# Two transformer blocks on one core: the raw residual stream is transposed, the norms' factors move to the weights and to the copies

## The reference

```
rms_norm(x, g) = x * rsqrt(mean(x * x) + 1e-6) * g
first block:  h = rms_norm(x, g_pre_mix);   proj = h @ w_in      (1024 x 3072)
              mix = [causal attention | gated retention] @ w_out
              x = x + rms_norm(mix, g_post_mix)
              c = cross_attention(rms_norm(x, g_pre_cross), rms_norm(mem, g_mem))
              x = x + rms_norm(c, g_post_cross)
              h = rms_norm(x, g_pre_ffn); gu = h @ w_gate_up; f = (silu(gate) * up) @ w_down  (2816 wide)
              x = x + rms_norm(f, g_post_ffn)
second block, layer 0: mix = [top-64 sparse attention chosen by an index | short convolution] @ w_out
              layer 1: mix = latent attention: q and kv pass through ranks 384 and 256 with norms of their own
              both:    x = x + rms_norm(mix, post);  x = x + rms_norm(relu(rms_norm(x, pre) @ w1)^2 @ w2, post)   (4096 wide)
```

## Time and profile before

| what | value |
|---|---|
| timed runs | 1163.12, 1163.36 and 1167.18 us, median 1163.36 |
| span of the profiled execution, first to last instruction | 1162.1 us |
| PE busy with products | 1066.5 us, 92% of the span |
| DVE, ACT, POOL busy | 638.6 (55%), 509.1 (44%), 99.7 us (9%) |
| mean granted clock of TensorE | 0.967 of full speed |
| PE on the chain that ended last | 73% |
| read from memory | 179.28 MB, 155 GB/s over the span |

### The profile page before, as it was taken

How to read it: one execution, slowest core, us unless ns; L and a number is a source line. 1 busy time by engine, 2 the same in 40 slices (tenths; PEclk the granted TensorE clock), 3 DMA queues, 4 the chain that set the end, 5 groups by cost and what they waited for, 6 DMA issues and landing times.

```text
span 1162.1 us, 13304 instructions
## 1 busy us (share of the span) xinstructions
PE 1066.5 (92%) x5072; PEld 886.6 (76%) x5072; DVE 638.6 (55%) x783; ACT 509.1 (44%) x637; POOL 99.7 (9%) x128
## 2 busy tenths in 40 slices
PE   5998899988999997899978799999878897999997
PEld 4887688776888886778867688888777776888886
DVE  4577663465554454457685655455545856454552
ACT  4556443344444444244444444444434644444441
POOL 1010110000000001102740000000140000000000
PEclk9999999998999999699989899999989998999999
DMA  8642274124545545434323545554154225455520
GB/s 340 249 182 91 74 263 170 73 91 163 201 162 191 205 158 179 144 147 144 145 72 109 197 166 183 197 192 150 52 175 150 74 86 188 179 180 183 188 100 36
DMA packets 29418, 180.92 MB, mean 156 GB/s; under 512 B 3520, under 2 KB 3904, under 8 KB 10816
## 3 DMA queue, kind: packets, MB, share of 16 engines
q1 hardware_dynamic: 26064, 170.08, 40.2%
q0 software_dynamic: 2592, 9.96, 2.5%
q10 hardware_dynamic: 720, 0.30, 0.1%
HBM read 179.28 MB, written 1.05 MB: 155 GB/s over the span
## 4 chain that ended last, share of the span: by engine, by line
PE 73%; DVE 12%; ACT 6%; POOL 5%; issue 3%; DMA 1%; POOLq 0%; DVEq 0%; ACTq 0%
PE PS L1257 63%; PE PS L1301 3%; DVE w_lo L827 3%; DVE h L905 3%; ACT w_hi L515 2%; PE PS L1346 2%; ACT work L576 2%; PE PS L1419 2%; PE PS L1329 2%; POOL h L431 1%; DVE x L920 1%; POOL rstd L408 1%; POOL msq L407 1%; DMA gain<-in_gains 1%; POOL arena L424 1%
## 5 line engine op out<-in xcount | busy, mean ns | idle before, releaser
L827 DVE TENSOR_TENSOR w_lo<-w_raw,w_hi 128x2048 fp32r<-128x2048 f32 (+3 forms) x177 | 369.1, 2096 | 317.3 <-ACT w_hi L515 316.9
L515 ACT ACTIVATE w_hi<-w_raw 128x2048 fp32r<-128x2048 f32 (+3 forms) x177 | 309.0, 1750 | 255.0 <-PE PS L1257 252.1
L1257 PE MATMUL PS<-w_hi,hT_hi 128*128 128x512 f32 (+3 forms) x904 | 323.1, 398 | 27.0 <-DVE hT_lo L843 17.7
L1257 PE MATMUL PS<-w_lo,hT_hi 128*128 128x512 f32 (+3 forms) x904 | 316.1, 391 | 0.0
L1257 PE MATMUL PS<-w_hi,hT_lo 128*128 128x512 f32 (+3 forms) x904 | 315.5, 390 | 0.0
L1257 PEld LDWEIGHTS PS<-w_hi,hT_hi 128*128 128x128 f32 x904 | 171.6, 194 | 64.3 <-issue 13.6
L1257 PEld LDWEIGHTS PS<-w_hi,hT_lo 128*128 128x128 f32 x904 | 173.6, 193 | 34.2
L1257 PEld LDWEIGHTS PS<-w_lo,hT_hi 128*128 128x128 f32 x904 | 174.1, 194 | 32.9
L1257 PE MATMUL PS<-w_hi,gT_hi 128*128 128x512 f32 x408 | 126.2, 391 | 0.6 <-DVE w_lo L827 0.6
L1257 PE MATMUL PS<-w_hi,gT_lo 128*128 128x512 f32 x408 | 125.7, 389 | 0.0
L1257 PE MATMUL PS<-w_lo,gT_hi 128*128 128x512 f32 x408 | 125.7, 389 | 0.0
(11 more groups left out here) (134 smaller groups left out, 739.4 us busy)
## 6 DMA issues: line engine op xcount, KB each, us to landing
w_raw<-in_w SPq DMA_DIRECT2D x64, 1024.0 KB, 4.8
w_raw<-in_w_gu SPq DMA_DIRECT2D x22, 1024.0 KB, 4.8
w_raw<-in_w_in SPq DMA_DIRECT2D x12, 1024.0 KB, 6.3
w_raw<-in_w_dn SPq DMA_DIRECT2D x22, 512.0 KB, 4.7
gain<-in_gains POOLq DMA_DIRECT2D x16, 512.0 KB, 4.8
w_raw<-in_w_out SPq DMA_DIRECT2D x4, 1024.0 KB, 4.8
w_raw<-in_w_mem_k SPq DMA_DIRECT2D x4, 1024.0 KB, 4.8
w_raw<-in_w_mem_v SPq DMA_DIRECT2D x4, 1024.0 KB, 4.8
```

Source lines behind the costliest of these rows:

```text
L515: act.activation(w_hi[:, u % RING, 0:size], w_raw[:, u % RAW, 0:size], ACT.Copy).then_inc(w_high, 1)
L827: dve.tensor_tensor(w_lo[:, u % RING, 0:size], w_raw[:, u % RAW, 0:size], w_hi[:, u % RING, 0:size].bitcast(F32), ALU.subtract).then_inc(w ...
L1257: mm = pe.matmul(bank(t, j)[:, 0:width], rows[:, kc0 + k, tok], w[:, s, at:at + width], start=begin and i == 0, stop=end and i == 2)
```

## The change

- The raw rows of `x` are transposed, 512 columns as soon as they are added up (`turn_stream`), not normed rows `h`. `normed` is gone, for `mem` too.
- A norm's gain is a factor of a row of the weights. The split multiplies by it: ACT's copy has it as a scale for each partition, DVE's subtraction becomes `(raw * gain) - hi`. Each block of 128 rows has its own column of gains in `gcol`, so a unit is split in `kcs` instructions: two of 1024 columns in most projections, four of 512 in the `up` units. Units without a norm before them (`w_out`, `w_co`, `w_dn` and their like) stay as they were.
- The 16 gains are loaded as 16 rows of one tile; PE transposes them at the start and ACT copies nine of them to `gcol`. The other seven, the gains behind a block, are still spread by POOL's queue.
- The reciprocal root is a factor of a token. It goes into the copies of the accumulators, into SiLU and ReLU as scale, and into the product of gate and up. These copies wait for `rstd_ready`.
- `add_to_stream` works in halves of 512 columns. In a boundary `high_rows` now comes before `stream_square`, and splits have other places between the steps.
- The start: SP loads x tile 0, half of the first unit, x tile 1, the other half; the first group has five units (1, 1, 2, 2, 2 blocks) and goes unit by unit over both tiles (`first_project`). The squares of x stand behind the first two splits.
- Behind a hidden layer the transposes of tile 0 stand ahead of the last part of its products; the transposes of tile 1 ahead of the fourth unit of the next projection, not behind it. The index queries now come before the index projection. The first `turn_hidden` of a layer stands between the second chunk's two units.
- The output is stored in four halves, not two tiles. `mem` is loaded ahead of `decay`.

```diff
-            def split(u, size, it=None):
+            def split(u, it=None):
...
-                act.activation(w_hi[:, u % RING, 0:size], w_raw[:, u % RAW, 0:size], ACT.Copy).then_inc(w_high, 1)
+                size, kcs, col = UNITS[u]
+                w = size // kcs
+                for k in range(kcs):
+                    ins = act.activation(w_hi[:, u % RING, k * w:(k + 1) * w], w_raw[:, u % RAW, k * w:(k + 1) * w], ACT.Copy,
+                                         scale=1.0 if col is None else gcol[:, col + TURNED * k:col + TURNED * k + 1])
+                ins.then_inc(w_high, 1)
...
+                    if col is None:
+                        ins = dve.tensor_tensor(lo, raw, hi, ALU.subtract)
+                    else:
+                        ins = dve.scalar_tensor_tensor(out=lo, in0=raw, scalar=gcol[:, col + TURNED * k:col + TURNED * k + 1], in1=hi,
+                                                       op0=ALU.mult, op1=ALU.subtract)
...
+            def add_to_stream(b, t):
...
+                dve.wait_ge(rstd_ready, stat + 1)
+                for i in range(2):
+                    cols = slice(512 * i, 512 * i + 512)
+                    steps.link(dve.scalar_tensor_tensor(out=h[:, t, cols], in0=PS[:, 2 * t + i, :], scalar=rstd[:, stat:stat + 1],
+                                                        in1=gain[:, g, cols], op0=ALU.mult, op1=ALU.mult))
+                    dve.tensor_tensor(x[:, t, cols], x[:, t, cols], h[:, t, cols], ALU.add).then_inc(x_ready, 1)
...
             def boundary_after(m):      # ACT
...
                 split_to(e + 1)
+                high_rows(hT_hi, 0)
                 stream_square(0)
-                high_rows(hT_hi, 0)
+                split_to(e + 2)
                 wait_acc(1)
                 square(acc(1))
-                split_to(e + 2)
-                stream_square(1)
                 split_to(e + 3)
                 high_rows(hT_hi, 1)
+                stream_square(1)
...
-            project(1, 8, [80], copies=2, rows=rows, hooks={(1, 0): tile1})
-            project(4, 2, wide, copies=2)
+            project(4, 2, wide, copies=2, rows=rows, hooks={(0, 3): tile1})
+            project(1, 8, [80], copies=2)
...
+            def turn_stream(t):
+
+                for half in range(2):
+                    n["x"] += 1
+                    pe.wait_ge(x_ready, n["x"])
+                    turn([x[:, t, P * (4 * half + b):P * (4 * half + b + 1)] for b in range(4)])
```

More of the change, by code:

```diff
@@ L49, with gained, plain_units, hidden_units @@
-SIZES, FIRST = [], {}
+GAINS = 16
+PRE_ROWS = [slice(0, 2), slice(3, 12, 2), slice(12, 15, 2)]
+PRE = {name: g for g, name in enumerate(["pre_mix", "mem", "pre_cross", "pre_ffn", "mix_pre0", "ffn_pre0", "mix_pre1", "ranks", "ffn_pre1"])}
+TURNED = len(PRE)
+def gained(gain, count, kcs, size):
+    return [(size, kcs, PRE[gain] + TURNED * j * kcs) for j in range(count)]
+def plain_units(count, size=2048):
+    return [(size, 1, None)] * count
+def hidden_units(gain, chunks, down):
+    up, down = gained(gain, 2, 4, 2048), plain_units(2, down)
+    return up + (up + down) * (chunks - 1) + down
@@ L50, with added @@
+UNITS, FIRST = [], {}
 for _name, _units in SCHEDULE:
[L51 to L56, removed]
+    FIRST[_name] = len(UNITS)
+    UNITS += _units
+COUNT = len(UNITS)
+POST = [2, 4, 6, 8, 10, 13, 15]
 GAIN_SLOTS = 2
+LATENTS = 4 + 4 * 5
+RETENTION = 34
+def added(b, t):
+    if b == 6:
+        return LATENTS + 8 + t
+    return 4 + 4 * b + 2 * t + (4 if b == 5 else 0)
@@ L343, in plain, with first_rows @@
                     for j in range(groups.shape[1]):
+                        if g == 0 and j < skip:
+                            continue
                         load(u, groups[g, j])
                         u += 1
+            def first_rows():
+                for t in range(TT):
+                    sp.dma_start(x[:, t, :], A["x"][:, t, :]).then_inc(x_loaded[t], 16)
+                    load(t, A["w_in"][0, 0][:, 1024 * t:1024 * (t + 1)])
             def hidden_layer(m):
@@ L552, in wait_acc, with group @@
                     act.wait_ge(w_used, n["used"])
-            def group(units, dsts, mid=None, ahead=3):
+            def group(units, dsts, stat, mid=None, ahead=3):
                 split_to(n["used"] + units - 1)
@@ L587, in half_rows, with boundary @@
                 return lambda i: (tile[:, chunk:chunk + 4, token_cols(i)], 4)
-            def boundary(units, whole=False):
+            def boundary(units):
                 split_to(n["used"] + 3)
@@ L1403, in up @@
                         mm.then_inc(w_used, 1)
+                        if first and j == 0:
+                            turn_hidden(c - 1)
                 def down(c, first, it=None):
```

451 lines of the change are left out of this document (239 added, 212 removed).

## The result

The changed kernel takes 1136.8 us in the median of four runs, the kernel before 1163.9 beside it: ratio 0.976, 95% interval 0.9745 to 0.9777. The forecast was 1138, range 1124 to 1155. The profiled execution spans 1133.2 us; its own timed value is 1135.0, 1.8 above that.

What follows compares the result with a forecast made beforehand. PE was taken to bound the layers' loops, so only its waits and the windows between loops could shrink. Terms +1.0 +0.3 -11.3 -12.5 -6.2 +1.5 +0.8 +0.2 = -26.2 from 1163.4 gave 1137, stated as 1138; range 1124 to 1155.

Steps and rivals of the forecast that it cites:

- The chain of a boundary: Between addition to x and transposes: second square, root and norm go, 4.3 us for each tile; x comes in halves.
- the three before the layers: Windows before the three hidden layers: 3.3, 4.4 and 3.6 us gained, sum -11.3, bounds 2 and 6 each.
- T0: Zero point of a boundary's timeline: the moment at which the first tile's accumulator is done.
- Behind layer 1: Window behind the first layer: 53.0 us become 40.5, -12.5, bounds -5 and -15.5; top-k stage +1.5 (0 to 3).
- Behind layer 2 and before layer 3: Behind the second layer -6.2 of 40.7 us, latent projections +0.8; before the third layer 3.6 gained.
- the start: Start of the kernel: products begin earlier, but a gap behind the first group gives that back; +1.0, bounds -3 and +4.
- the gap behind the first group: At the start, PE idles from 35.7 to 40.3, about 4.6 us, as no next unit is split ahead of the sine.
- The end: Kernel's end: four short instructions for two, +0.4, less what a half-size last store saves; +0.2 taken.
- (a): Rival: the clock doesn't fall in the shorter gaps, runs of small products disappear, 9 us more gained: 1128; chance 0.17.
- (b): Rival: PE waits for ACT's and DVE's chains, some 10 gained splits come about 1 us later: 1148; chance 0.24.
- (c): Rival: the split with a column factor runs at half rate, 4.6 us a unit, +53: 1190; chance 0.05.
- (d): Rival: the gain moves into the top-k stage and the start, nothing is left: 1160; chance 0.07.

Runs made afterwards that it cites:

- experiment 3: Changed kernel with square, root and norm of x put back between addition and transposes, new split order kept: 1185.1 us, ratio 1.018.
- experiment 5: Changed kernel, norm gone, but ACT's and DVE's splits and ACT's squares of x in the order of the kernel before: 1144.3 us, ratio 0.984.
- experiment 6: Changed kernel with the norm put back and the splits in the order of the kernel before: 1167.6 us, ratio 1.003.
- experiment 1: Changed kernel with the sixth unit of weights split ahead of the first group's copies, not behind the sine: 1131.7 us, ratio 0.973.
- experiment 7: Changed kernel, but PE waits for both halves of x before it transposes the first: 1136.8 us.
- experiment 9: Experiment 1's edit on the changed kernel, plus each layer's first hidden rows ahead of the fifth unit's split on ACT and DVE: 1119.1 us, ratio 0.961.
- experiment 10: Experiment 9, and at the start ACT splits the third and fourth unit ahead of its squares of x: 1114.5 us, ratio 0.958.

## Why the prediction was right, and where it was off

**The chain of a boundary.** Right in sign and size. At the boundaries 20.3 us of waits for the normed rows became 3.9 for x. The prediction worked out each boundary in its new order as a whole and didn't part the norm from the order of the splits; experiments 3, 5 and 6 do. For the three before the layers it had -11.3, measured were -14.0. In the second and third, PE stood at the second chunk 2.2 us earlier than forecast. About half is POOL, in the timeline of the second tile:

```profile
631.17 0.41 POOL L462 TENSOR_SCALAR msq<-ssq 128x1 f32<-128x1 f32 x1 [2.62 <-ACT work L637]
631.66 0.94 POOL L463 TENSOR_TENSOR rstd<-msq,neg_half 128x1 f32<-128x1 f32 x1
```

The root beside four pieces of DVE's split comes at T0+15.7, not 16.8: the steps take 0.41 and 0.94 in place of 0.19 and 0.55 where DVE runs no split (at 627.72 and 628.00), but nothing like the 1.98 of the earlier trace rows. The other half is the clock: the forecast had the second tile's 24 products end at T0+29, some of them at the lower clock; they ended at T0+26.7, all at the full one. The Trainium skill ("SBUF — State Buffer", Who interferes with whom) has the shared ports locked for one instruction at a time; by that rule shorter pieces hold POOL up more briefly, and the trace agrees.

**Behind layer 1.** -12.5 and +1.5 predicted, -11.6 measured, with one error in each direction. Rows at T0+9.5 (9.0 predicted). PE was at the lower clock twice, 13.2 us of busy time in these two windows:

```profile
458.40:465.30 6.90, 6.27 (x16) 4.42 (x16) 5.55 (x7) 6.77 (x9) 2.49 (x4) 0.51 0.47 156
489.10:496.00 6.90, 6.90 (x28) 6.37 (x28) 4.59 (x8) 3.35 (x9) 0.00 (x0) 0.51 0.92 322
```

If all that work would run twice as fast at the full clock, they cost 6.6, where I had taken 3.0. Experiments 1, 7, 9 and 10 leave this part of the program as it is or nearly so, 5 changes the splits' places, and all their profiles are shorter in this stage, by 1.6 (experiment 10) to 3.6: the clock was down there for 3.4 us in experiments 1, 5 and 9, for twice 3.4 in 7, for 6.9 in 10. So the match of -11.6 with -11.0 is in part luck: with fewer falls the stage would have come out 2 to 4 us below the forecast.

**Behind layer 2 and before layer 3.** -9.0 predicted for the two with the latents, -13.5 measured. In the first, idle time alone gave the 6.2 that were forecast for its boundary, the 0.8 added for the latents did not appear, and busy time gave 1.7 more; in the second busy time gave 2.8. The clock is behind most of it: before, PE was busy for 8.8 and 5.8 us at the lower clock in these two stages, after for 6.7 and 0, which at half the rate is 1.1 and 2.9.

**The term that was mis-sized: the start, +1.0 with bounds -3 and +4, measured +5.5.** The order of events was as forecast, the gap behind the first group too: 4.77 us of idle time where 4.6 was worked out. Its rows, PE, ACT and DVE:

```profile
12.81 0.73 PE L1325 MATMUL PS<-w_hi,hT_hi 128*128 128x512 f32 x2 [1.37 <-DVE w_lo L919]
...
20.38 0.73 PE L1325 MATMUL PS<-w_hi,hT_hi 128*128 128x512 f32 x2 [1.84 <-DVE w_lo L919]
...
43.38 1.19 PE L1325 MATMUL PS<-w_hi,hT_hi 128*128 128x512 f32 x2 [4.77 <-DVE w_lo L919]
...
37.07 1.28 ACT L772 ACT_TABLE_LOAD   x1
38.36 0.28 ACT L772 ACTIVATE trig<-work 128x96 f32<-128x96 f32 x1
38.55 6.33 ACT L568 ACTIVATE w_hi<-w_raw,gcol 128x1024 fp32r<-128x1024 f32 x6
...
40.75 4.87 DVE L919 SCALAR_TENSOR_TENSOR w_lo<-w_raw,gcol,w_hi 128x1024 fp32r<-128x1024 f32 x4 [13.01 <-ACT w_hi L568]
```

The rows of gains landed at 6.86, where their transposes were put at 5.5; the first product came at 12.81 and the third unit at 20.38, for 19.3. Up to 48.8 us the clock fell twice, where the forecast had one fall:

```profile
42.00:48.80 6.80, 5.42 (x13) 4.29 (x14) 6.80 (x7) 5.96 (x6) 0.00 (x0) 0.50 0.98 354
21.50:24.90 3.40, 3.40 (x10) 2.62 (x9) 3.40 (x4) 0.47 (x1) 0.00 (x0) 0.50 0.85 347
```

8.8 us of busy PE at half clock cost 4.4, against 1.4 in the sum. Against the forecast's own times the 4.5 us come together thus: the third unit 1.1 later; the last 72 products 18.2 us long and not 16.4, with the first fall among them; the gap 0.2 longer; and 2.7 for the second fall in place of 1.4. The table says the same from the other side: of the +5.5, PE's idle time is 0.6, its busy time 4.9. (A third fall, from 96.6 to 100.0, has its like in the kernel before, from 91.4 to 94.9.)

One fall comes behind the wait of 1.84, the other with that of 4.77; experiment 10, without the first wait and with 1.97 for the second, has none in the start. But experiment 1 has the first wait too, 1.80 at 20.09, and no fall behind it, and the changed kernel has the same wait before layers 2 and 3:

```profile
645.93 0.56 PE L1325 MATMUL PS<-w_hi,hT_hi 128*128 128x512 f32 x1 [2.36 <-DVE arena L1073]
...
955.10 0.47 PE L1325 MATMUL PS<-w_hi,hT_hi 128*128 128x512 f32 x1 [2.37 <-DVE arena L1073]
```

Behind the first the clock is at 0.50 from 646.2 to 649.6, behind the second it stays at 1.00 (955.0 to 960.0). So in these runs fewer waits go with fewer falls; that a given wait brings one isn't shown, and its length alone doesn't decide it. The Trainium skill ("TensorE: Matmul & The Clock Gate", What's actually happening) has an idle array lose half its rate until activity restores it. The rows agree in the size of the fall, 0.50, and in part in the cause: a fall behind 2.36, none behind 2.37.

**The end.** -0.3 for +0.2. The last addition ends at T0+13.1 in place of 12.8, so the four short instructions cost 0.3, not 0.4; from there to the end it is 2.4 us in place of 3.0. The stores themselves take 2.0 us for 256 KB and 2.6 for 512 KB in the two traces. By the Trainium skill ("DMA: Bandwidth & Descriptors", Anatomy of one DMA) the estimate was 0.6 saved and -0.2 in all. The Trainium skill gives that sum for transfers that POOL issues, and these are SP's; the difference between the two sizes, 0.6, is what the traces show.

**The rivals.** (a), a clock that doesn't fall in the shorter gaps, isn't the changed kernel, whose clock is at its lower level for 43.3 us; experiment 10 comes near it with 15.2. (b) did not come: outside the start PE's waits for splits are 7.9 us, before the change at most 8.5, and those for x and the low rows fell. (c) is out: a split takes 2.44 or 2.74, not 4.6. (d) has one true part, the start, which gave back 5.5.

The total came out so close because the errors cancel: the start was 4.5 us dearer than its term, all other stages together 7.1 cheaper than theirs. The clock has a part in both.

## What to carry to other kernels

Take a step off a chain and its engines' orders can change too: here the norm's removal was worth 23 us as the orders stood and some 8 more by moving splits into the time that it freed, while the same moves with the norm in place cost 17. After such a change read again what stands ahead of each step that PE waits for: two small moves, the unit of the next group split ahead and the hidden rows ahead of a split, gave 18 us more between the medians (15 between the profiles), and a third, at the start, 5. A good part of that is the clock. Compare stages by PE's idle and busy time apart, since a short wait also shows up as slower products behind it.

## What the runs showed of the hardware

- PE's busy time for the same products ran from 1066.5 us (before) over 1059.2 (changed) to 1045.4 (experiment 10), with the clock at its lower level for 77.6, 43.3 and 15.2 us of the spans. PE was busy for 57.3, 38.6 and 10.3 of these. If all that work would run twice as fast at the full clock, half the difference between the first two, 9.3, is an estimate of what the clock gave: a third of the whole gain. The busy time itself fell by 7.4, with 1.0 added by the transposes of the gains.
- A gained split takes 2.44 us in two pieces and 2.74 in four on DVE, against 2.29 for the subtraction in one; on ACT four pieces take 2.56 against 1.92 in one.
- The same program differs in how long its clock is down from execution to execution: the changed kernel's four runs have spans of 1133.2, 1133.7, 1136.4 and 1136.6 with mean clocks of 0.981, 0.981, 0.976 and 0.976.
- A load of the gains of 16 rows, issued at 1.2 us among the first transfers, was there for PE at 6.9.
- Two waits of PE for the same instruction, 2.36 and 2.37 us long, in one execution: the clock fell behind the first and not behind the second.
